# One matmul of 128 columns for two products with the same left side, transposes in place of some products with the identity, and a new step list, in a two-block transformer kernel

## The chip, the cores and the metric
The kernel runs on one core of one Trainium2 chip. The metric is the device time of one execution in microseconds (us).

## The reference
Two blocks run one after the other over 512 tokens of 1024 features in float32. The first block mixes a windowed pool with gated linear attention and has a squared-ReLU MLP. The second block has a causal convolution beside an RWKV-7 recurrence, then cross-attention to 256 memory rows, then a SwiGLU MLP. The change touches the recurrence only:

```
s_kk = einsum("bhvk,bhk->bhv", S, kk_t)
S = S * w_t[:, :, None, :] - s_kk[..., None] * (kk_t * a_t)[:, :, None, :] + v_t[..., None] * k_t[:, :, None, :]
y_t  = einsum("bhvk,bhk->bhv", S, r_t)          # 8 heads of 64, 512 steps
```

It feeds `y = concat([y_conv, y_rwkv]) @ w_out`, and the convolution has 31 taps over 512 channels.

## The kernel before
**Dense products.** All weights come as one stream of units. ScalarE rounds a unit to a high part (`wh`), VectorE takes the rest (`wl`), and every dense 128x512 product is three matmuls (`wh` by high, `wh` by low, `wl` by high). A step `mm` is half of the k range of one output tile: 12 matmuls (6 in units 76 and 77, the `wa` units). These show as `ps<-zr,wh` and `ps<-zr,wl`.

**The recurrence in chunks.** The 512 steps are 8 chunks of 64. Heads go in four pairs hp = 0 to 3; a pair has two heads (hh) on partitions 0-63 and 64-127. For each pair four groups of steps run:
- `prep.*` builds scaled keys and values. Its `prep.turn` (three steps of four 128x128 transposes) waits for the scaled arrays nB, K and P. They come from `prep.scale` and `prep.shift` on VectorE and ScalarE.
- `head.*` takes five products per chunk, each 64x64 on 64 rows: `a` (nB by P), `aa` (P by nB), `pk` (K by P), `rt` (K by R), `qt` (nB by R). VectorE masks four of them out of PSUM. Then a triangular inverse is built in five levels: `head.x` and `head.z` (64x64 by 64x32 matmuls with a VectorE op after each) and `head.tz`, which turns Z by a product with the identity (`ident`, shown as `ps<-cf_sb,zf 64*64`), after which ScalarE copies it out. Each such step is 16 matmuls, one per chunk and head; `ps<-zf 64*64` matmuls on partitions (row half, column half) of the array run four at a time. `head.gh` multiplies the inverse by two right sides, 32 matmuls.
- `fin.*` carries the state over the chunks (`fin.m`, `fin.n`, then six short dependent `fin.s`) and normalizes.
- The convolution taps: `tap.v` is one 128x512 VectorE op in PSUM (61 of them), `tap.g` a ScalarE multiply and a GpSimd add.

**What sets the order.** Each engine issues its instructions in the order of one list of steps. The list is made by `schedule()`: dense steps come in a fixed order, and at every stop the string `TURNS` says which background generator goes next (c conv taps on VectorE, g taps on GpSimd, p prep, h head pairs 0 and 2, i head pairs 1 and 3, f fin, o the `wa` and `wb` products). A dot ends the turns at one stop. After the last `p` tile (step `mm 75,1,13,1`) no dense product is left until the `wa` units. This part between them is called the bare stretch below. Steps wait on semaphores for the results that they read and for PSUM banks to be free. Background steps share five or six banks.

Every float32 matmul (not `fp32r`) is two instructions in the trace, a transpose is one. Thus a `head` step of 16 matmuls is x32 there.

Of the kernel before, what the change touches and what calls it, by code (L numbers as in the profile page):

```python
# [21 lines left out]
TURNS = """  # L22
...ppp...pp.p.p.pp.pggggp.pppp.hhggg..ccgghhcccggg.hcccc..gcc.cggghggghgccccgcc.hcccc.hcggggg.cc.hc.
h.hghc.pcghgpgpcpc..pgchcc.gpphgg.ghcc.pccpcpp.hccg..c.ghhg.hc.cpppppihggppfffgcfcffcigicpfigciciifc
pfgggiciiipicgfgiicggfcicppfpifipppcicfcpphchhhcfhhgiiggphifihhgppffffghcgghpccffchhgfcfchfcfcppfhcc
pfpchpchcfhfppcphfphpfchiicihicifiififfifcfififcfiifcicfioofiiooofooifiioiofifooffffffofofoofoofoofo
foofoofooofofoooooooo
"""
# [16 lines left out]
RO = [24, 25, 26, 27]  # L45
KS = [28, 29, 30, 31]
# [304 lines left out]
def schedule():  # L351
# [330 lines left out]
    def bg_head(z):  # L682
        for hp in (z, z + 2):
            while not has(("prep", hp)) or (z and not has(("pdone",))) or (hp >= 2 and not has(("fin", hp - 2))):
                yield

            def one(what, *more):
                for hh in range(2):
                    pl.take("M", "head." + what, hp, hh, *more)
                put("head." + what, hp, *more)  # L690
                for hh in range(2):
                    pl.rel("M", "head." + what, hp, hh, *more)
            put("head.zi", hp)
# [24 lines left out]
            yield  # L718
# [313 lines left out]
def program(nc, wstream, vecs, cf, cu, xT, metaT, memT, pmix, gup, wau, gupg, out, x2s, kvs):  # L1032
# [5 lines left out]
    with ctx:  # L1038
# [16 lines left out]
        dsm3 = sb("dsm3", [P, 24])  # L1055
        cuts = [0, 8, 24, 34, 47, 55, 75]

# [71 lines left out]
        def freed(*key):  # L1129
            k = pl.before[key]  # L1130
            if k and k[0] in ("fin.y1", "fin.yc"):
                return k[0:2]
            if k and k[0] in DIRECT:
                return DIRECT[k[0]]
            if k and k[0] == "xr.t":
                return ("xr.s", k[1][0:2], 7, 1)
            return k

# [72 lines left out]
        def cat_hl(i):  # L1211
            return R(CS[i]), R(47 + i)

        def prep_bufs(hp):

            z = hp % 3
            return (*[F(i) for i in [(3, 5, 7, 2), (4, 6, 52, 59), (21, 72, 73, 74)][z]], dsm3[:, 8 * z:8 * z + 8])

        def head_bufs(hp, hh):
            m, rest = [[(53, 54, 61, 70), (10, 11, 14, 16)], [(55, 60, 62, 63), (12, 13, 15, 17)]][hh][hp % 2], [71, 18][hp % 2]  # L1220
            (AT, AA), (Z, T), (RT, QT) = [(F(i)[:, 0:256], F(i)[:, 256:512]) for i in m[0:3]]
            return AT, AA, Z, T, F(rest)[:, 256 * hh:256 * hh + 256], RT, QT, F(m[3])

        def later(x, lv):
# [118 lines left out]
        def prods(hp):  # L1343
            return [("mm", "head." + w_, hp - 1, hh) for w_ in ("pk", "qt") for hh in range(2)] if hp else []

# [14 lines left out]
        def tensor(e):  # L1360
# [229 lines left out]

            def prod(what, lhs, rhs, hp):
                K = "head." + what
                for hh in range(2):
                    e.wait_ge(freed(K, hp, hh), *prep_done(hp))
                for _, rows_, cs, bl in CHUNKS:
                    t = [e.mm(ps(K, hp, hh)[rows_, bl], lhs[hs, cs], rhs[hs, cs]) for hh, hs in enumerate(HALVES)]
                    if bl.stop == 256 and rows_.stop == 128:
                        done2(t, K, hp)

            def head_a(hp):  # L1600
                prod("a", nB, Pp, hp)

            def head_pk(hp):
                prod("pk", F(KS[hp]), Pp, hp)

            def head_rt(hp):
                prod("rt", F(KS[hp]), F(RO[hp]), hp)

            def head_qt(hp):
                prod("qt", nB, F(RO[hp]), hp)  # L1610

            def head_aa(hp):
                prod("aa", Pp, nB, hp)
# [43 lines left out]
            def head_gh(hp, hh):  # L1657
                s0 = 64 * hh
                _, _, Z, _, PX, _, _, _ = head_bufs(hp, hh)
                b, Pt = ps("head.gh", hp, hh), prep_bufs(hp)[3]  # L1660
                e.wait_ge(freed("head.gh", hp, hh), ("head.z", hp, hh, 5), ("head.px", hp, hh))
                for a, rows_, _, bl in CHUNKS:
                    t = e.mm(b[rows_, a * 128:a * 128 + 64], Z[rows_, bl], Pt[rows_, a * 128 + s0:a * 128 + s0 + 64])
                for a, rows_, _, bl in CHUNKS:
                    t = e.mm(b[rows_, a * 128 + 64:a * 128 + 128], Z[rows_, bl], PX[rows_, bl])
                t.then_inc(*e.up("mm", "head.gh", hp, hh))

            def fin_y1(hp):
# [4 lines left out]
                for a, rows_, _, bl in CHUNKS:  # L1673
                    for hh in range(2):
                        _, _, _, _, _, _, QT, GH = head_bufs(hp, hh)
                        t = e.mm(ps("fin.y1", hp, rows_.start // 64)[64 * hh:64 * hh + 64, bl],
                                 GH[rows_, a * 128:a * 128 + 64], QT[rows_, bl])
                t.then_inc(*e.up("mm", "fin.y1", hp))
# [4 lines left out]
            def fin_m(hp):  # L1683
# [3 lines left out]
                for a, par, hh in STATE:  # L1687
                    hs, ts_, GH = HALVES[hh], HALVES[par], head_bufs(hp, hh)[7]
                    t = e.mm(ps("fin.m", hp, par)[hs, a * 64:(a + 1) * 64], GH[ts_, a * 128:a * 128 + 64],
                             nBt[ts_, a * 128 + hs.start:a * 128 + hs.stop])  # L1690
# [3 lines left out]
            def fin_n(hp):  # L1694
# [3 lines left out]
                for a in range(4):  # L1698
# [5 lines left out]
                    for par, hh in now:  # L1704
                        kc = slice(a * 128 + 64 * hh, a * 128 + 64 * hh + 64)
                        t = e.mm(ps("fin.n", hp, par)[HALVES[hh], a * 64:(a + 1) * 64], nBt[HALVES[par], kc],
                                 head_bufs(hp, hh)[7][HALVES[par], a * 128 + 64:a * 128 + 128], start=False)
                        if (a, hh) == (3 - par, 1):
# [11 lines left out]
            def fin_yc(hp):  # L1720
# [6 lines left out]
                for a, rows_, _, bl in CHUNKS:  # L1727
# [3 lines left out]
                    for hs, _, QT, GH in two:  # L1731
                        t = e.mm(o[hs, bl], GH[rows_, a * 128 + 64:a * 128 + 128], QT[rows_, bl], start=False)
                t.then_inc(*e.up("mm", "fin.yc", hp))
# [42 lines left out]
            def att_out(g, d):  # L1776
# [11 lines left out]
                "prep.gates": prep_gates, "prep.norm": prep_norm, "prep.kn": prep_kn, "prep.vmm": prep_vmm,  # L1788
                "prep.turn": prep_turn, "head.a": head_a, "head.pk": head_pk, "head.rt": head_rt, "head.qt": head_qt,
                "head.aa": head_aa, "head.tz": head_tz, "head.x": head_x, "head.z": head_z, "head.px": both(head_px),  # L1790
# [368 lines left out]
        def vector(e):  # L2159
# [317 lines left out]

            def masked(what, buf, m, hp, hh):
                K = ("head." + what, hp, hh)
                e.wait_ge(("mm", *K), *two_back(hp))  # L2480
                e.tt(c64(buf), c64(ps(*K)[:, 0:256]), half4(m), MUL).then_inc(*e.up(*K))

            def head_a(hp, hh):
                K = ("head.a", hp, hh)
                e.wait_ge(("mm", *K), ("head.zi", hp, hh))
                e.raw.copy_predicated(c64(head_bufs(hp, hh)[2]), half4("u0"), c64(ps(*K)[:, 0:256])).then_inc(*e.up(*K))

            def head_pk(hp, hh):
                masked("pk", head_bufs(hp, hh)[7][:, 0:256], "lt", hp, hh)

            def head_rt(hp, hh):
                masked("rt", head_bufs(hp, hh)[5], "le", hp, hh)

            def head_qt(hp, hh):
                masked("qt", head_bufs(hp, hh)[6], "le", hp, hh)

# [488 lines left out]
```

## Time and profile before

| | |
|---|---|
| runs (3) | 1672.67, 1674.36, 1677.11 us; median 1674.36 |
| profiled execution, its own time | 1673.94 us |
| its span, first to last instruction | 1672.0 us |
| TensorE busy (PE) | 1607.8 us, 96% |
| VectorE busy (DVE) | 820.1 us, 49% |
| ScalarE / GpSimd busy | 606.5 / 397.8 us |
| mean granted TensorE clock | 0.981 of full |

A busy PE here includes the tail of each matmul, so 96% is not 96% of its peak. The shares are means over stages; the recurrence takes about 270 of the 1672 us.

### The profile page before, as it was taken

The page shows a single profiled execution, that of the slowest core. Times are in us where ns is not written, and L with a number is a line of the kernel's source. Part 1 is how long each engine was busy: PE and PEld are TensorE (multiplying, and loading weights), DVE is VectorE, ACT ScalarE, POOL GpSimd, SP SyncE. Part 2 cuts the span into 40 slices and gives each one's busy share as a digit, 9 for nine tenths or more (in the row PEclk, how much of TensorE's full clock was granted, in tenths as well). Part 3 has the DMA queues.
Part 4 walks back from the last instruction along what each step waited for, and adds up shares of the span by engine and source line. Part 5 has one row for each costly group of instructions (what it writes and reads, how often), then busy time and mean ns, then how long its engine had stood idle before and what let it go on. Part 6 is the DMA issues. An engine that isn't in the chain of part 4 may idle for free.

```text
span 1672.0 us, 26892 instructions
## 1 busy us (share of the span) xinstructions
PE 1607.8 (96%) x11510; PEld 1316.6 (79%) x11510; DVE 820.1 (49%) x1240; ACT 606.5 (36%) x981; POOL 397.8 (24%) x333
## 2 busy tenths in 40 slices
PE   6999999999999999999999987898999999999997
PEld 5888877787888888888877766778879888888876
DVE  3376842344533333334479987637536432333334
ACT  4134432333431313234345554425335322222222
POOL 2012201302220201013317443105003430230233
PEclk8899999999999999999999999899999999999998
DMA  5122412123222222222242100014203222222212
GB/s 204 51 102 95 163 72 68 59 101 123 104 86 94 98 101 79 98 101 89 76 151 77 53 27 4 5 51 177 76 25 102 76 101 101 79 99 101 94 64 69
DMA packets 29829, 146.03 MB, mean 87 GB/s; under 512 B 4096, under 2 KB 7440, under 8 KB 14608
## 3 DMA queue, kind: packets, MB, share of 16 engines
q1 hardware_dynamic: 29712, 144.33, 24.5%
q8 instruction: 91, 1.49, 0.4%
q14 instruction: 26, 0.21, 0.0%
HBM read 138.03 MB, written 6.29 MB: 86 GB/s over the span
## 4 chain that ended last, share of the span: by engine, by line
PE 80%; issue 7%; DVE 7%; POOL 3%; ACT 2%; DMA 0%; POOLq 0%; SPq 0%; DVEq 0%
PE ps L169 79%; POOL zf L181 2%; DVE zf L181 2%; DVE ps L189 2%; DVE wl L181 1%; DVE zf L189 1%; DVE zr L189 1%; PE ps L172 1%; ACT zf L175 0%; POOL tn L181 0%; ACT zr L178 0%; DMA raw<-in_wstream 0%; ACT zf L178 0%; ACT wh L178 0%; ACT muh L178 0%
## 5 line engine op out<-in xcount | busy, mean ns | idle before, releaser
L169 PE MATMUL ps<-zr,wh 128*128 128x512 f32 (+1 forms) x3936 | 1164.5, 380 | 14.6 <-DVE wl L181 9.6
L169 PEld LDWEIGHTS ps<-zr,wh 128*128 128x128 f32 x3936 | 711.3, 188 | 170.6 <-DVE wl L181 9.8
L169 PE MATMUL ps<-zr,wl 128*128 128x512 f32 (+1 forms) x1968 | 741.6, 377 | 0.0
L181 POOL TENSOR_TENSOR zf<-zf 128x512 f32<-128x512 f32 (+1 forms) x237 | 287.8, 1220 | 804.1 <-ACT zf L175 553.4
L169 PEld LDWEIGHTS ps<-zr,wl 128*128 128x128 f32 x1968 | 370.5, 188 | 76.2
L181 DVE TENSOR_TENSOR wl<-raw,wh 128x1024 fp32r<-128x1024 f32 (+1 forms) x243 | 308.7, 1310 | 209.8 <-ACT wh L178 209.6
L178 ACT ACTIVATE wh<-raw 128x1024 fp32r<-128x1024 f32 (+1 forms) x243 | 240.4, 1038 | 211.9 <-PE ps L169 211.2
L175 ACT ACTIVATE zf<-zf 128x512 f32<-128x512 f32 (+2 forms) x232 | 127.4, 560 | 375.8 <-DVE zf L181 261.5
L181 DVE TENSOR_TENSOR zf<-ps,zf 128x512 f32<-128x512 f32 (+2 forms) x165 | 97.6, 597 | 191.9 <-PE ps L169 166.5
L169 PE MATMUL ps<-zf 64*64 64x64 f32 (+6 forms) x3768 | 167.6, 245 | 21.8 <-issue 9.8
L169 PEld LDWEIGHTS ps<-zf 64*64 64x64 f32 (+3 forms) x3768 | 131.9, 148 | 61.6 <-issue 37.3
L181 POOL TENSOR_TENSOR zr<-zf,zr 128x512 fp32r<-128x512 f32 x54 | 70.2, 1301 | 280.3 <-ACT zr L178 280.3
L178 ACT ACTIVATE zf<-ps 128x256 f32<-128x256 f32 (+2 forms) x160 | 72.6, 484 | 161.7 <-PE ps L169 149.2
L181 DVE TENSOR_TENSOR zf<-zf,ps 128x512 f32<-128x512 f32 (+2 forms) x112 | 56.5, 522 | 136.1 <-PE ps L169 135.7
L178 ACT ACTIVATE zr<-zf 128x512 fp32r<-128x512 f32 x74 | 46.6, 632 | 158.0 <-POOL zf L181 140.9
L189 DVE SCALAR_TENSOR_TENSOR zf<-ps,zf 128x512 f32<-128x512 f32 x46 | 31.5, 690 | 93.2 <-PE ps L169 87.7
L181 POOL TENSOR_TENSOR tn<-tn,cf_sb 128x2 f32<-128x2 f32 (+3 forms) x29 | 33.2, 1145 | 174.9 <-DVE tn L185 95.8
L178 ACT ACTIVATE zf<-zf,vecs_sb 128x512 f32<-128x512 f32 x73 | 50.9, 719 | 44.3 <-DVE zf L181 23.2
L189 DVE SCALAR_TENSOR_TENSOR ps<-zf,vecs_sb,ps 128x512 f32<-128x512 f32 (+1 forms) x93 | 61.0, 656 | 3.2 <-PE ps L169 2.4
L189 DVE SCALAR_TENSOR_TENSOR zr<-zf,vecs_sb,zr 128x256 fp32r<-128x256 f32 (+1 forms) x64 | 45.3, 740 | 32.5 <-ACT zr L178 32.5
L181 DVE TENSOR_TENSOR zf<-zf 128x512 f32<-128x512 f32 (+4 forms) x75 | 53.0, 720 | 10.2 <-ACT zf L175 9.8
L169 PE MATMUL ps<-cf_sb,zf 64*64 64x64 f32 (+2 forms) x860 | 43.4, 236 | 9.8 <-POOL zf L181 6.3
(95 smaller groups left out, 693.7 us busy)
## 6 DMA issues: line engine op xcount, KB each, us to landing
raw<-in_wstream SPq DMA_DIRECT2D x117, 1024.0 KB, 4.8
zf<-in_xT SPq DMA_DIRECT2D x16, 256.0 KB, 3.0
raw<-in_wstream SPq DMA_DIRECT2D x4, 768.0 KB, 4.5
kv_scratch<-zf SPq DMA_DIRECT2D x8, 256.0 KB, 2.2
x_scratch<-zf SPq DMA_DIRECT2D x8, 256.0 KB, 2.1
zf<-x_scratch SPq DMA_DIRECT2D x8, 256.0 KB, 4.1
out<-zf SPq DMA_DIRECT2D x16, 128.0 KB, 1.7
zf<-in_cu SPq DMA_DIRECT2D x1, 1256.0 KB, 10.1
```

What stands on the lines that cost most here:

```text
L169: return self.raw.matmul(out_, l, x, start=start, stop=stop)
L172: return self.raw.transpose(out_, in_, idn)
L175: return self.raw.activation(out_, in_, fn, bias=bias, scale=scale)
L178: return self.raw.activation(out_, in_, mybir.ActivationFunctionType.Copy, scale=scale)
L181: return self.raw.tensor_tensor(out_, a, b, o)
L189: return self.raw.scalar_tensor_tensor(out=out_, in0=a, scalar=s, in1=b, op0=o1, op1=o2)
```

## The change
1. `prod` now gives 128 columns for two right sides that lie in two buffers: `a` also yields `qt` (both nB on the left), `pk` also yields `rt` (both K on the left). The moving operand reads 64 columns of P and 64 of R (`beside`). VectorE masks read columns 0-63 or 64-127 of each chunk of the same bank, which is held until both masks are done. `aa` stays.
2. `head.gh` does its two right sides as one matmul of 128 columns over two buffers, 16 matmuls in place of 32. Buffers of the pairs move to make the distances positive.
3. In `head.tz` the 8 of 16 products whose output lies on partitions 0-63 become transposes.
4. `TURNS` is new. Nothing else changes in the work: masks, copies and taps are the same in number and size.

```diff
-            one("a")
-            yield
-            one("aa")
-            yield
-            one("pk")
-            yield
+            yield from two("a", "qt")
+            yield from two("pk", "rt")
+            mark("prodq", hp)
...
-                if lv < 4:
-                    one(("rt", "qt", "px")[lv - 1])
                 if lv == 2:
-                    mark("prodq", hp)
-                if lv < 4:
+                    one("px")
                     yield
...
+        def beside(c0, c1, rows_, at_=0):
+
+            x = ZF[:, c0 + at_:c0 + at_ + 64][rows_, :]
+            return bass.AP(x.tensor, x.offset, [x.ap[0], [c1 - c0, 2], x.ap[-1]])
...
             def prod(what, lhs, rhs, hp):
+
                 K = "head." + what
                 for hh in range(2):
                     e.wait_ge(freed(K, hp, hh), *prep_done(hp))
-                for _, rows_, cs, bl in CHUNKS:
-                    t = [e.mm(ps(K, hp, hh)[rows_, bl], lhs[hs, cs], rhs[hs, cs]) for hh, hs in enumerate(HALVES)]
+                for a, rows_, cs, bl in CHUNKS:
+                    to = slice(128 * a, 128 * a + 128) if len(rhs) == 2 else bl
+                    t = [e.mm(ps(K, hp, hh)[rows_, to], lhs[hs, cs],
+                              beside(*rhs, hs, cs.start) if len(rhs) == 2 else rhs[0][hs, cs])
+                         for hh, hs in enumerate(HALVES)]
...
-                    t = [e.mm(ps(K, hp, hh, lv)[HALVES[h ^ hh], bl], head_bufs(hp, hh)[2][rows_, bl],
-                              ident[rows_, rows_]) for hh in range(2)]
+                    t = [(e.mm if h ^ hh else e.tr)(ps(K, hp, hh, lv)[HALVES[h ^ hh], bl],
+                                                     head_bufs(hp, hh)[2][rows_, bl], ident[rows_, rows_])
+                         for hh in range(2)]
...
-                for a, rows_, _, bl in CHUNKS:
-                    t = e.mm(b[rows_, a * 128:a * 128 + 64], Z[rows_, bl], Pt[rows_, a * 128 + s0:a * 128 + s0 + 64])
-                for a, rows_, _, bl in CHUNKS:
-                    t = e.mm(b[rows_, a * 128 + 64:a * 128 + 128], Z[rows_, bl], PX[rows_, bl])
+                    x = (PT[hp] * 512 + a * 128 + 64 * hh, PXS[hp % 2] * 512 + 256 * hh + 64 * a)
+                    t = e.mm(b[rows_, a * 128:a * 128 + 128], Z[rows_, bl], beside(min(x), max(x), rows_))
```

The first line of `TURNS` before and now, of five:

```diff
-...ppp...pp.p.p.pp.pggggp.pppp.hhggg..ccgghhcccggg.hcccc..gcc.cggghggghgccccgcc.hcccc.hcggggg.cc.hc.
+...ppp..p..p.pp..ppp.p...cgggcccccgcpggpg.ggccpccpc..cgc.ggcchhggggh.cchch.gg.ccgghgccc.ggh.hc.ccggh
```

On TensorE, where the transposes of pair 0 (`prep.turn`, line 172) end and its first head products follow, before:

```order
L169 MATMUL ps<-zr,wl 128x512
L172 MATMUL ps<-cf_sb,zf 128x128 x12
L169 MATMUL ps<-zr,wh 128x512 x2
L169 MATMUL ps<-zr,wl 128x512
L169 MATMUL ps<-zr,wh 128x512 x2
```

and now at the place of pair 0's transposes:

```order
L172 MATMUL ps<-cf_sb,zf 128x128 x8
L169 MATMUL ps<-zr,wh 128x512 x2
L169 MATMUL ps<-zr,wl 128x512
L169 MATMUL ps<-zr,wh 128x512 x2
L169 MATMUL ps<-zr,wl 128x512
L169 MATMUL ps<-zr,wh 128x512 x2
L169 MATMUL ps<-zr,wl 128x512
L169 MATMUL ps<-zr,wh 128x512 x2
L169 MATMUL ps<-zr,wl 128x512
L172 MATMUL ps<-cf_sb,zf 128x128 x4
```

The third `prep.turn` stood directly behind the second; a dense half step of 12 matmuls lies between them now, and the transposes start three dense half steps later in the program.

On TensorE at the start of the bare stretch (the head products of pair 1 with `head.gh`, `fin.m`, `fin.n`, `fin.y1` and `fin.yc` of pair 0), before:

```order
L169 MATMUL ps<-zf 64x32 x16
L172 MATMUL ps<-cf_sb,zf 128x128 x12
L169 MATMUL ps<-zf 128x512 x2
L169 MATMUL ps<-zf 64x64 x172
L169 MATMUL ps<-cf_sb,zf 128x2 x4
```

and now:

```order
L169 MATMUL ps<-zf 64x32 x16
L172 MATMUL ps<-cf_sb,zf 128x128 x4
L169 MATMUL ps<-zf 128x512 x2
L169 MATMUL ps<-zf 64x128 x16
L169 MATMUL ps<-zf 64x64 x16
L169 MATMUL ps<-zf 64x128 x16
L169 MATMUL ps<-zf 64x64 x14
L169 MATMUL ps<-zf 64x128 x16
L172 MATMUL ps<-cf_sb,zf 64x64
L169 MATMUL ps<-cf_sb,zf 64x64 x2
L172 MATMUL ps<-cf_sb,zf 64x64 x2
```

Eight of the twelve transposes are gone from here to an earlier place. The products are 16 of 128 columns (`a` with `qt`), 16 of 64 (`aa`), 16 of 128 (`head.gh` of pair 0), 14 of 64 (`fin.m`), 16 of 128 (`pk` with `rt`); the last rows are `head.tz`, in which transposes (line 172) and products (line 169) alternate. `fin.n`, `fin.y1` and `fin.yc` come later.

On TensorE at the first dense products behind the bare stretch (`wa`, unit 76), before:

```order
L169 MATMUL ps<-zf 64x32 x16
L169 MATMUL ps<-cf_sb,zf 64x64 x16
L169 MATMUL ps<-zr,wh 128x512 x2
L169 MATMUL ps<-zr,wl 128x512
L169 MATMUL ps<-zr,wh 128x512 x2
L169 MATMUL ps<-zr,wl 128x512
L169 MATMUL ps<-zf,cf_sb 128x512
```

and now, at the end of the first dense tile:

```order
L172 MATMUL ps<-cf_sb,zf 64x64
L169 MATMUL ps<-zr,wh 128x512 x2
L169 MATMUL ps<-zr,wl 128x512
L169 MATMUL ps<-zr,wh 128x512 x2
L169 MATMUL ps<-zr,wl 128x512
L169 MATMUL ps<-zf 64x32 x16
L169 MATMUL ps<-zf 64x64 x16
L169 MATMUL ps<-zr,wh 128x512 x2
L169 MATMUL ps<-zr,wl 128x512
L169 MATMUL ps<-zr,wh 128x512 x2
L169 MATMUL ps<-zr,wl 128x512
L169 MATMUL ps<-zf,cf_sb 128x512
```

These rows are `head.z` 3 of pair 3, `fin.y` of pair 2, dense products, and `fin.mu` of pair 2. Before, pair 3 had done its levels up to `head.x` 4 and pair 2 its `fin.y` when the dense products began. Now they begin after `head.z` 2 of pair 3 and `fin.s` 5 of pair 2, so three more level steps, two turns, `fin.s` 6 and `fin.y` lie between dense products.

## Rows read from the trace of the kernel before

**Rows 1.** The page's head: span, and busy time of each engine with its instructions.

```profile
span 1672.0 us, 26892 instructions
PE 1607.8 (96%) x11510; PEld 1316.6 (79%) x11510; DVE 820.1 (49%) x1240; ACT 606.5 (36%) x981; POOL 397.8 (24%) x333
```

**Rows 2.** Windows over the recurrence: stretch, its length, then busy time by engine.

```profile
core 0: us, PE busy (x) PEld busy (x) DVE busy (x) ACT busy (x) POOL busy (x), PEclk, DMA share, GB/s
847.90:875.00 27.10, 24.78 (x128) 19.68 (x126) 19.95 (x26) 11.12 (x17) 7.90 (x5) 0.98 0.25 88
875.00:903.80 28.80, 28.80 (x354) 22.56 (x352) 22.72 (x33) 18.13 (x30) 19.53 (x14) 0.96 0.22 75
903.80:950.90 47.10, 46.22 (x506) 35.16 (x498) 44.57 (x68) 26.49 (x44) 30.95 (x19) 1.00 0.19 68
950.90:960.60 9.70, 9.70 (x108) 7.70 (x100) 8.93 (x14) 3.95 (x6) 1.30 (x1) 1.00 0.01 2
963.60:1080.20 116.60, 94.48 (x3006) 79.14 (x3005) 91.22 (x213) 57.43 (x121) 37.88 (x28) 0.93 0.02 5
1080.20:1103.70 23.50, 23.50 (x459) 18.50 (x456) 10.96 (x26) 9.51 (x19) 1.64 (x1) 1.00 0.14 48
1103.70:1118.00 14.30, 14.30 (x100) 10.40 (x96) 3.69 (x7) 5.12 (x8) 0.00 (x0) 1.00 0.19 74
```

**Rows 3.** Waits of TensorE in the bare stretch: us in total, times, longest.

```profile
PE ps L169 <- issue: 9.6, 10, 1.8
```

**Rows 4.** Timeline around pair 0's transposes, 868 to 876 us.

```profile
868.71 4.89 POOL L181 TENSOR_TENSOR zf<-zf 128x512 f32<-128x512 f32 x3
869.14 3.34 DVE L181 TENSOR_TENSOR zf<-zf 128x512 f32<-128x512 f32 x2
...
874.21 1.11 PE L172 MATMUL ps<-cf_sb,zf 128*128 128x128 f32 x4 [2.32 <-DVE zf L181]
```

**Rows 5.** Windows in which the granted clock was half: columns of rows 2.

```profile
873.80:877.20 3.40, 2.99 (x9) 2.57 (x10) 0.95 (x2) 2.41 (x5) 0.00 (x0) 0.52 0.01 5
986.60:993.30 6.70, 5.96 (x179) 5.89 (x182) 4.69 (x12) 1.13 (x4) 1.92 (x2) 0.50 0.01 2
1048.10:1054.80 6.70, 6.70 (x93) 5.53 (x92) 3.43 (x8) 2.20 (x4) 3.03 (x2) 0.50 0.01 2
1065.20:1068.30 3.10, 3.10 (x114) 3.10 (x110) 1.31 (x6) 0.00 (x0) 0.00 (x0) 0.50 0.02 5
```

**Rows 6.** Timeline of TensorE: dense products, then `head.pk` and `head.tz` of pair 0.

```profile
877.52 0.63 PE L169 MATMUL ps<-zr,wh 128*128 128x512 f32 x2
...
878.22 0.63 PE L169 MATMUL ps<-zr,wh 128*128 128x512 f32 x2
...
885.58 0.40 PE L169 MATMUL ps<-zr,wl 128*128 128x512 f32 x1
885.90 0.69 PE L169 MATMUL ps<-zf 64*64 64x64 f32 x32
886.42 0.65 PE L169 MATMUL ps<-cf_sb,zf 64*64 64x64 f32 x32
```

**Rows 7.** Timeline of TensorE, first block: four 64x64 products of 128 columns.

```profile
246.20 0.65 PE L169 MATMUL ps<-zf 64*64 64x128 f32 x8
246.78 0.50 PE L169 MATMUL ps<-zr,wh 128*128 128x512 f32 x1
```

**Rows 8.** Timeline of TensorE: full-array transposes and the product behind them.

```profile
864.81 0.60 PE L172 MATMUL ps<-cf_sb,zf 128*128 128x128 f32 x4
865.17 0.72 PE L169 MATMUL ps<-zr,wh 128*128 128x512 f32 x2
```

**Rows 9.** Groups of VectorE by form, 846 to 1118 us: busy us, mean ns.

```profile
L189 DVE SCALAR_TENSOR_TENSOR ps<-zf,vecs_sb,ps 128x512 f32<-128x512 f32 x61 | 45.7, 749 | 0.8
L181 DVE TENSOR_TENSOR zf<-ps,cu_sb 128x128 f32<-128x128 f32 x40 | 9.7, 283 | 1.9 <-PE ps L169 1.6
L181 DVE TENSOR_TENSOR zf<-zf,ps 128x128 f32<-128x128 f32 x40 | 9.6, 280 | 5.6 <-PE ps L169 5.5
```

More of the change, by code:

```diff
@@ L693, in bg_head, with two @@
             put("head.zi", hp)
-            one("a")
-            yield
-            one("aa")
-            yield
-            one("pk")
-            yield
+            def two(what, more):
+                for hh in range(2):
+                    pl.take("M", "head." + what, hp, hh)
+                put("head." + what, hp)
+                yield
+                if what == "a":
+                    one("aa")
+                    yield
+                put("head." + more, hp)
+                for hh in range(2):
+                    pl.rel("M", "head." + what, hp, hh)
+                yield
+            yield from two("a", "qt")
+            yield from two("pk", "rt")
+            mark("prodq", hp)
             one("tz", 0)
@@ L1055, in program @@
         dsm3 = sb("dsm3", [P, 24])
-        cuts = [0, 8, 24, 34, 47, 55, 75]
+        cuts = [0, 28, 34, 47, 55, 75]
         class Zone:
@@ L1136, in freed @@
                 return ("xr.s", k[1][0:2], 7, 1)
+            if k and k[0] in ("head.a", "head.pk"):
+                return ({"head.a": "head.qt", "head.pk": "head.rt"}[k[0]], *k[1:])
             return k
@@ L1343, in prods @@
         def prods(hp):
-            return [("mm", "head." + w_, hp - 1, hh) for w_ in ("pk", "qt") for hh in range(2)] if hp else []
+            return [("mm", "head." + w_, hp - 1, hh) for w_ in ("a", "pk") for hh in range(2)] if hp else []
         def both(step):
@@ L1657, in head_gh @@
             def head_gh(hp, hh):
[L1658 removed]
                 _, _, Z, _, PX, _, _, _ = head_bufs(hp, hh)
                 b, Pt = ps("head.gh", hp, hh), prep_bufs(hp)[3]
[L1661 removed]
+                e.wait_ge(freed("head.gh", hp, hh), ("head.px", hp, hh), ("head.z", hp, hh, 5))
                 for a, rows_, _, bl in CHUNKS:
[L1663 to L1665 removed]
+                    x = (PT[hp] * 512 + a * 128 + 64 * hh, PXS[hp % 2] * 512 + 256 * hh + 64 * a)
+                    t = e.mm(b[rows_, a * 128:a * 128 + 128], Z[rows_, bl], beside(min(x), max(x), rows_))
                 t.then_inc(*e.up("mm", "head.gh", hp, hh))
@@ L1688, in fin_m @@
                     hs, ts_, GH = HALVES[hh], HALVES[par], head_bufs(hp, hh)[7]
-                    t = e.mm(ps("fin.m", hp, par)[hs, a * 64:(a + 1) * 64], GH[ts_, a * 128:a * 128 + 64],
+                    t = e.mm(ps("fin.m", hp, par)[hs, a * 64:(a + 1) * 64], GH[ts_, g_at(hp, a)],
                              nBt[ts_, a * 128 + hs.start:a * 128 + hs.stop])
@@ L1706, in fin_n @@
                         t = e.mm(ps("fin.n", hp, par)[HALVES[hh], a * 64:(a + 1) * 64], nBt[HALVES[par], kc],
-                                 head_bufs(hp, hh)[7][HALVES[par], a * 128 + 64:a * 128 + 128], start=False)
+                                 head_bufs(hp, hh)[7][HALVES[par], h_at(hp, a)], start=False)
                         if (a, hh) == (3 - par, 1):
@@ L1731, in fin_yc @@
                     for hs, _, QT, GH in two:
-                        t = e.mm(o[hs, bl], GH[rows_, a * 128 + 64:a * 128 + 128], QT[rows_, bl], start=False)
+                        t = e.mm(o[hs, bl], GH[rows_, h_at(hp, a)], QT[rows_, bl], start=False)
                 t.then_inc(*e.up("mm", "fin.yc", hp))
@@ L1788, in tensor @@
                 "prep.gates": prep_gates, "prep.norm": prep_norm, "prep.kn": prep_kn, "prep.vmm": prep_vmm,
-                "prep.turn": prep_turn, "head.a": head_a, "head.pk": head_pk, "head.rt": head_rt, "head.qt": head_qt,
+                "prep.turn": prep_turn, "head.a": head_a, "head.pk": head_pk,
                 "head.aa": head_aa, "head.tz": head_tz, "head.x": head_x, "head.z": head_z, "head.px": both(head_px),
@@ L2476, in prep_shift, with masked @@
                 e.tt(Pp, kkv, TD, MUL).then_inc(*e.up("prep.P", hp))
[L2478 to L2481, printed above, removed]
+            def masked(what, of, at_, buf, m, hp, hh):
+                e.wait_ge(("mm", of, hp, hh), *two_back(hp))
+                e.tt(c64(buf), every(ps(of, hp, hh), at_), half4(m), MUL).then_inc(*e.up("head." + what, hp, hh))
             def head_a(hp, hh):
```

39 lines of the change are left out of this document (21 added, 18 removed).

## Prediction

> **What bounds the kernel now.** I read the head of the page first. TensorE is busy 1607.8 of the 1672.0 us, VectorE 820.1 us [rows 1]. The dense stages before and after the recurrence are not touched by the change, so the question is the recurrence, 847.9 to 1118 us. The windows cut it at the steps where both programs can be compared [rows 2]:
>
> - 847.9 to 875 us: dense products with the preparation of pair 0. TensorE is busy 24.78 of 27.10 us.
> - 875 to 903.8: dense, TensorE busy throughout, VectorE 22.72 of 28.80.
> - 903.8 to 950.9: dense, but VectorE is busy 44.57 of 47.10 us. VectorE is as much the bound here as TensorE.
> - 963.6 to 1080.2: the bare stretch, 116.60 us. TensorE is busy 94.48 and VectorE 91.22. Neither is full: small products and masks wait for each other. TensorE is idle 22.1 us, of which 9.6 us has no visible releaser [rows 3].
> - 1080.2 to 1118: the `wa` products. TensorE is busy all 23.50 and 14.30 us, VectorE 10.96 and 3.69.
>
> Two losses stand out. At 874.21 us the third transpose of pair 0 starts after 2.32 us of waiting for VectorE. Its inputs are late because two VectorE ops took 3.34 us together while GpSimd ran its taps (4.89 us from 868.71) [rows 4]. And in four places the granted clock was at half, the lower level of 1.2 GHz, 19.9 us together; the first place starts in that very idle time [rows 5].
>
> **Part 1, the merged products.** Sixteen products of 64 columns are 32 instructions, and from the start of `head.pk` to the start of `head.tz` behind it pass 0.52 us (885.90 to 886.42) [rows 6]. Four array quarters work side by side, so that is eight rounds of 0.065. What 128 columns cost on such a quarter stands in the first block: eight instructions on two quarters, four rounds, are 0.58 us ahead of the next dense product (246.20 to 246.78) [rows 7]. A switch of shape costs 0.09 us: dense start to 64x64 start is 0.32 us (885.58 to 885.90), where dense products follow each other at 0.70 / 3 = 0.233 [rows 6]. Without it a round of 128 columns is (0.58 - 0.09) / 4 = 0.12 us, with it 0.145; I take 0.115 to 0.12. So twice the columns cost nearly twice the time, and the number of instructions hardly counts. Per pair, before: five products of 0.52 = 2.6 us. Now: two of 8 x 0.12 = 0.95 and one of 0.52, 2.4 us. That saves 0.2 us per pair, 0.8 for four. If 128 columns cost no more than 64, it would be 1.04 per pair, 4.2 in all; at 0.145 it is a loss of 0.24 per pair, 1.0 in all. `head.gh` has 64 instructions on two quarters at a time, 32 rounds of 0.06 = 1.9 us, now 16 of 0.115 = 1.8: 0.3 us for four pairs. One or two groups less per pair between dense products save a switch of 0.09 each, 0.3 us in all. Part 1 gives **-1.4 us**.
>
> The VectorE masks are the same in number and elements and read with a stride: 0. PSUM banks are now held from the product to the second mask, which the new list must bear. If it doesn't, TensorE waits some tenths of a us for a bank. I count it in the range.
>
> **Part 2, transposes in `head.tz`.** A step is 32 instructions, in eight rounds [rows 6]. Eight of its 16 products become single instructions, so it has 24. But those on output partitions 64-127 stay products of two instructions, four on each of their two quarters: eight rounds, 0.52 us, as before. The quarters work side by side, so the transposes only shorten the two that don't end last. I take **0**. A gain of a quarter of 0.52 us, 0.13 for each of 20 steps, 2.6 us, would need the time to follow the number of instructions, which Part 1's rows speak against. The bound on the other side is a rival (below).
>
> **Part 3, the new list.** I follow the stretches.
>
> - 847.9 to 875: the three transposes of pair 0 come three dense half steps later, and the GpSimd taps start behind `prep.shift`. The 2.32 us wait has cover now: a half step is 12 x 0.233 = 2.8 us. The half clock that follows an idle TensorE [rows 5] costs up to 1.7 us; with 9 dense and transposing instructions in it I take 1.2. **-3.5 us**. If the wait comes back elsewhere: 0.
> - 875 to 903.8: 19 taps in place of 22; TensorE is the bound. 0.
> - 903.8 to 950.9: 24 taps in place of 18, six of 0.75 us = 4.5 us more on VectorE [rows 9], which had 2.5 us left. **+3.0 us** is taken (between +2.0, the overflow, and +4.5). What then waits is the dense step that needs a freed bank or a mask of `head.x` behind the taps.
> - 950.9 to 963.6: two of pair 1's transposes move here, eight transposes at 0.36 / 4 = 0.09 us or a little over, **+0.9 us** with a switch, on a full TensorE [rows 8].
> - The bare stretch: out of it go two transpose steps, `head.x` 3, `head.z` 3, `head.x` 4 and two `head.tz` of pair 3, `fin.s` 6 and `fin.y` of pair 2, and on VectorE four taps. TensorE: 0.9 + 5 x 0.5 + 1.1 = 4.5 us, less. VectorE: 4 x 0.75, six ops of 0.28 = 1.7, and about 1.0 for `fin.s` and `fin.y`, 5.7 us less of 91.22 [rows 9]. Where both take turns, the stretch follows the larger of the two: 5.7 / 91.22 x 116.6 = 7.3; purely by TensorE 4.5. I take **-6.5 us**, the saving of part 1 aside.
> - 1080.2 to 1118: the five level steps, `fin.y` and `fin.s` 6 go to where TensorE is full: 2.5 + 1.1 = **+3.5 us**, since they displace nothing idle.
>
> Hidden at no cost is the later start of pair 0's products, by dense steps; if that cover failed, pair 0 would be late for `head.gh` and the bare stretch would start with a wait of about 1 to 3 us.
>
> Sum: -1.4 + 0 - 3.5 + 3.0 + 0.9 - 6.5 + 3.5 = -4.0. The profiled execution took 1673.94 us, which gives 1669.9; the median of the runs is 0.4 higher, and I forecast **1670 us** (1665 to 1674 for this case alone).
>
> **Rivals.**
>
> *The bare stretch tightens more.* Its 22.1 us of idle TensorE and its 16.5 us at half clock [rows 2, 3, 5] are there to be won, and the order within it is new throughout. If half of the idle time and one more half-clock place go, 10 us more: **1660**. For it: neither engine is full. Against: chains of `fin.s` and the levels are as long as before, and each link needs a TensorE step, a VectorE op and two hand-overs.
>
> *The list only moves work.* The stretch keeps its length, because the chain of the levels sets it and not VectorE's sum; the dense stretches pay as above. -1.4 - 3.5 + 3.0 + 0.9 + 0 + 3.5 = +2.5: **1677**. Against it speaks VectorE at 78% of the stretch.
>
> *The transposes cost a switch each (the slower side).* In `head.tz` products and transposes now alternate, eight changes in each of 20 steps, 160 in all. If TensorE must empty at each, the nearest price is 0.09 us, that of going from full-array to 64x64 work [rows 6]: 160 x 0.09 = 14.4, so **1684**. It decides the sign from about 0.03 us a change, where it eats the 4 us. Against: in the full array the dense product behind four transposes starts 0.36 us after the first of them (864.81 to 865.17), which leaves no room for a gap [rows 8]. No row shows it for quarters. The Trainium skill speaks for this rival: "TensorEngine Tiling (Array Packing)", under Restrictions and Gotchas, says that column tiling and the transpose mode for FP32 input exclude each other on TRN2, and under Key Properties that changing the tiling mode drains TensorE. By that rule, with a gap at each change, the sum would be that of this rival; no row here shows a transpose on a quarter.
>
> **How the numbers follow.** A measurement of this kernel can tell about 0.3%, 5 us, from no change. Chances: forecast 0.43, tighter 0.20, only moved 0.22, switches 0.15. The band for same is 1669.3 to 1679.4. Faster: all of the tighter case and half of the forecast, 0.42. Slower: the switches and a little of the moved case, 0.18. Same: 0.40. The range goes from 1657 (tighter, with Part 1's and Part 2's upper gains cut) to 1684, the middle of the slow case, and leaves 0.15 outside.
>
> **What would show it.** In the profile after: TensorE has 10966 instructions (384 fewer by the merging, 160 by the transposes; if not, the change isn't what the code says). A 64x128 group of 32 takes about 0.95 us to the next start (0.52: columns are free). A `head.tz` group keeps 0.65 us (above 1 us: the switches; 0.5: the count of instructions rules). No wait of 2.3 us before a third transpose and no half clock behind it. The stretch 903.8 to 950.9 longer by 3, with waits for VectorE in dense steps. The bare stretch near 109 us. `wa` to `kt` 41 in place of 37.8. The forecast is wrong if the bare stretch keeps 116 us, or loses over 12, or if `head.tz` grows.

## The result, and the profile after

The changed kernel takes 1692.85 us (median of 4 runs, 1690.36 to 1694.72), the kernel before 1675.49 (4 runs, 1672.67 to 1677.11): 1.0096 of its time, 95% interval 1.008 to 1.0112. That is 16 us slower; the forecast was 1670, and 1684 was the end of the range.

The head of the page of the changed kernel, which answers to [rows 1]:

```profile
span 1688.4 us, 25801 instructions
PE 1636.6 (97%) x10966; PEld 1332.2 (79%) x10966; DVE 824.6 (49%) x1240; ACT 606.8 (36%) x981; POOL 395.5 (23%) x333
```

TensorE has the 10966 instructions that were foretold, 544 fewer, and is busy 28.8 us longer. So its work has become dearer. Windows over the recurrence, cut at the same steps as [rows 2] (columns of that group):

```profile
847.37:870.37 23.00, 23.00 (x115) 18.19 (x114) 14.41 (x22) 8.37 (x12) 2.40 (x2) 1.00 0.32 111
870.37:896.88 26.51, 26.51 (x205) 21.24 (x203) 25.06 (x31) 17.39 (x28) 17.82 (x13) 1.00 0.24 80
896.88:953.74 56.86, 55.49 (x567) 40.95 (x563) 51.44 (x76) 30.89 (x52) 36.27 (x25) 0.97 0.17 57
969.66:1085.73 116.07, 104.22 (x2418) 81.86 (x2417) 85.74 (x202) 55.38 (x116) 32.66 (x24) 0.91 0.01 4
1085.73:1117.07 31.34, 31.34 (x526) 23.58 (x524) 9.66 (x25) 9.15 (x18) 1.64 (x1) 0.97 0.11 35
1117.07:1133.20 16.13, 16.13 (x174) 11.63 (x168) 6.12 (x17) 4.77 (x9) 0.00 (x0) 1.00 0.20 67
```

The first stretch lost 4.1 us, the second 2.3. The third grew by 9.8, and the short one behind it (up to 966.67, the head of the next dense half step) by 3.2. The bare stretch is as long as before (116.07 against 116.60), with 588 matmuls fewer in it and 9.7 us more of busy TensorE. The `wa` stretches grew by 9.7 us together. Where this comes from shows in the timeline of TensorE at the first `head.tz` of pair 0, which answers to the `head.tz` row of [rows 6]:

```profile
902.35 0.39 PE L169 MATMUL ps<-zr,wl 128*128 128x512 f32 x1
902.67 0.24 PE L172 MATMUL ps<-cf_sb,zf 64*64 64x64 f32 x1
902.84 0.33 PE L169 MATMUL ps<-cf_sb,zf 64*64 64x64 f32 x4
903.11 0.24 PE L172 MATMUL ps<-cf_sb,zf 64*64 64x64 f32 x2
903.28 0.33 PE L169 MATMUL ps<-cf_sb,zf 64*64 64x64 f32 x4
903.54 0.25 PE L172 MATMUL ps<-cf_sb,zf 64*64 64x64 f32 x2
903.72 0.33 PE L169 MATMUL ps<-cf_sb,zf 64*64 64x64 f32 x4
903.98 0.25 PE L172 MATMUL ps<-cf_sb,zf 64*64 64x64 f32 x2
904.16 0.33 PE L169 MATMUL ps<-cf_sb,zf 64*64 64x64 f32 x4
904.42 0.24 PE L172 MATMUL ps<-cf_sb,zf 64*64 64x64 f32 x1
904.59 0.73 PE L169 MATMUL ps<-zr,wh 128*128 128x512 f32 x2
```

Line 172 is a transpose, line 169 a product. From the first transpose to the dense product behind the step pass 1.92 us, against some 0.6 before. One pair of changes takes 0.44 us (902.67 to 903.11, 903.11 to 903.54), where two rounds took 0.12. Summed over the 20 steps, the time from the first to the last start of a step is 36.7 us, against 11.1 before.

### The profile page after: what moved, and what is told of

The parts are those of the page before. It is cut to its first block, busy times and chain, and to the rows that moved or that the text cites. A ratio compares the mean times of both kernels' runs of the same rounds, so it can differ in the third digit from the quotient of the medians.

```text
span 1688.4 us, 25801 instructions
## 1 busy us (share of the span) xinstructions
PE 1636.6 (97%) x10966; PEld 1332.2 (79%) x10966; DVE 824.6 (49%) x1240; ACT 606.8 (36%) x981; POOL 395.5 (23%) x333
## 4 chain that ended last, share of the span: by engine, by line
PE 81%; issue 7%; DVE 7%; POOL 3%; ACT 2%; DMA 0%; POOLq 0%; SPq 0%; DVEq 0%; ACTq 0%
PE ps L169 79%; POOL zf L181 2%; DVE zf L181 2%; DVE ps L189 2%; PE ps L172 2%; DVE zf L189 1%; DVE wl L181 1%; DVE zr L189 1%; ACT zr L178 0%; ACT zf L175 0%; POOL tn L181 0%; ACT wh L178 0%; DMA raw<-in_wstream 0%; ACT zf L178 0%; DVE zr L181 0%
## 5 line engine op out<-in xcount | busy, mean ns | idle before, releaser
L181 DVE TENSOR_TENSOR wl<-raw,wh 128x1024 fp32r<-128x1024 f32 (+1 forms) x243 | 314.0, 1332 | 208.3 <-ACT wh L178 208.2
L169 PE MATMUL ps<-zf 64*64 64x32 f32 (+8 forms) x3384 | 165.2, 254 | 15.8 <-DVE zf L181 6.2
L169 PEld LDWEIGHTS ps<-zf 64*64 64x64 f32 (+3 forms) x3384 | 128.4, 149 | 57.5 <-issue 32.8
L178 ACT ACTIVATE zf<-ps 128x512 f32<-128x512 f32 (+2 forms) x160 | 73.5, 484 | 190.0 <-PE ps L169 175.6
L169 PE MATMUL ps<-cf_sb,zf 64*64 64x64 f32 (+2 forms) x540 | 56.6, 252 | 9.4 <-POOL zf L181 6.9
L169 PEld LDWEIGHTS ps<-cf_sb,zf 64*64 64x64 f32 (+1 forms) x540 | 45.2, 164 | 17.8 <-POOL zf L181 9.3
```

The costliest lines, as they stand in the source:

```text
L169: return self.raw.matmul(out_, l, x, start=start, stop=stop)
L178: return self.raw.activation(out_, in_, mybir.ActivationFunctionType.Copy, scale=scale)
L181: return self.raw.tensor_tensor(out_, a, b, o)
```

## The experiments

All times are medians; each ratio is against the kernel before in the same comparison (its medians 1676.4 to 1677.9 us). The four kernels of the first comparison take the change apart.

**1. The products back.** Of the changed kernel only the transposes are undone:

```diff
-                    t = [(e.mm if h ^ hh else e.tr)(ps(K, hp, hh, lv)[HALVES[h ^ hh], bl],
-                                                     head_bufs(hp, hh)[2][rows_, bl], ident[rows_, rows_])
-                         for hh in range(2)]
+                    t = [e.mm(ps(K, hp, hh, lv)[HALVES[h ^ hh], bl], head_bufs(hp, hh)[2][rows_, bl],
+                              ident[rows_, rows_]) for hh in range(2)]
```

> The changed kernel with all sixteen turns of each inverse step as products again; merged products and the new step list stay. Theory (each change between transpose and product costs): a turning step falls from 1.92 to about 0.6 us, 20 of them are 26 us less work on TensorE; some of it lay where TensorE waited anyway, so 1692.9 falls to 1668 to 1674 us. Rival (the new list or the merged products lose the time and the long turning steps lie beside waits): 1685 to 1693 us.

Measured: 1674.05 us, 0.9979 (0.9969 to 0.9988). The transposes alone make the difference between 0.9979 and 1.0096, 19.6 us (18.8 between the medians). Its `head.tz` at the same place, on TensorE's timeline, takes 0.62 us again:

```profile
903.45 0.69 PE L169 MATMUL ps<-cf_sb,zf 64*64 64x64 f32 x32
904.07 0.73 PE L169 MATMUL ps<-zr,wh 128*128 128x512 f32 x2
```

**2. The transposes alone.** The kernel before, with the same edit of `head.tz` the other way round.

> The kernel before with the transposes in its turning steps as the only edit. Theory: 20 steps times 1.3 us is 26 us more; the bare stretch before has 22 us of idle TensorE that may hide some, so 1675.5 rises to 1692 to 1702 us, more than the whole change did. Rival (list or merging is to blame): 1675 to 1680 us.

Measured: 1690.59 us, 1.0082 (1.0069 to 1.0095), 13.8 us slower, a little under what was expected. The steps sum to 37.5 us from first to last start, 26.4 more than before. TensorE's waits between 847 and 1135 us are 12 us in all, against 24 before, so nearly half of the added work fell into time in which it had been idle.

**3. Transposes first, then products.**

```diff
+                for op, d in ((e.tr, 0), (e.mm, 1)):
+                    for a in range(4):
+                        t = []
+                        for hh in range(2):
+                            h = hh ^ d
+                            rows_, bl = HALVES[h], slice(64 * a, 64 * a + 64)
+                            t.append(op(ps(K, hp, hh, lv)[HALVES[h ^ hh], bl],
+                                        head_bufs(hp, hh)[2][rows_, bl], ident[rows_, rows_]))
```

> The changed kernel with the eight transposes of a turning step first and the eight products behind them: two changes of kind in a step in place of eight or nine, the same instructions. If a change of kind costs 0.16 us: a step takes 0.24 us for the transposes, 0.47 for the products on two quarters and 0.3 for two changes, about 1.0 us, and the time is 1674 to 1681 us. If each 64-column transpose is slow by itself: the step stays near 1.9 us and the time near 1692 us.

Measured: 1679.6 us, 1.0011 (1.0003 to 1.002). One change in a step in place of eight; timeline of TensorE:

```profile
903.82 0.41 PE L172 MATMUL ps<-cf_sb,zf 64*64 64x64 f32 x8
904.17 0.68 PE L169 MATMUL ps<-cf_sb,zf 64*64 64x64 f32 x16
904.78 0.74 PE L169 MATMUL ps<-zr,wh 128*128 128x512 f32 x2
```

The step takes 0.95 us, still 0.33 more than products alone, so the number of changes isn't the whole price. In this order the transposes would stand in rounds of their own in any case; that the two kinds don't run side by side shows where they alternate. There a product starts 0.17 us after the transposes ahead of it (903.11 to 903.28), while in experiment 1 four products start within 0.02 us of each other.

**4. The list alone.** Experiment 1 with each product of 128 columns issued as two of 64 in its place, `head.gh` too:

```diff
+                    if len(rhs) == 2:
+                        for m in range(2):
+                            t = [e.mm(ps(K, hp, hh)[rows_, 128 * a + 64 * m:128 * a + 64 * m + 64], lhs[hs, cs],
+                                      ZF[:, rhs[m] + cs.start:rhs[m] + cs.start + 64][hs, :])
+                                 for hh, hs in enumerate(HALVES)]
```

> As the first of these (turns as products, new list), but each merged product of 128 columns is two of 64 columns into the same places of the bank, for the head products and for the inverse times its right sides. So only the new list is left of the change. If time goes with columns: 0.92 us for a merged group against 1.0, 1.70 against 1.86 for the inverse, 0.3 us per pair and 1.4 us in all more than the first run. If the number of instructions counts: 4 us or more above the first run.

Measured: 1676.4 us, 0.9998 (0.999 to 1.0007). The new list by itself gives nothing, and the merging on it 2.3 us, between the two expectations. With intervals of 0.1% (some 1.6 us) on each side, it can't be told from 1.4.

**5. The merging alone, on the old list.** `TURNS` is that of before; `head.qt` and `head.rt` are masks directly behind `head.a` and `head.pk`:

```diff
+            def two(what, more):
...
+                put("head." + what, hp)
+                put("head." + more, hp)
...
+            two("a", "qt")
             yield
-            one("a")
```

> The list of steps of the kernel before, head.tz as products, and only the merged products (head.a with head.qt, head.pk with head.rt, head.gh as one of 128 columns); each second mask stands directly behind the first. This is Part 1 alone. By the runs so far (the merging took 2.3 us off the new list) it should be 1.4 to 2.5 us under the kernel before, with five products of 0.52 us per pair replaced by two of 0.93 and one of 0.52. Rival: the bank that is now held for two masks makes TensorE wait on the old list, and the time is that of before or up to 2 us more.

Measured: 1670.32 us, 0.9956 (0.9942 to 0.997). That is 6.9 us faster, three to five times what was expected, so something else than columns is at work here.

**6 and 7. Transposes only where TensorE is full, or only where it isn't.** The changed kernel, with transposes in the 8 steps between dense products (below), or in the other 12 (the condition without its `not`):

```diff
-                    t = [(e.mm if h ^ hh else e.tr)(ps(K, hp, hh, lv)[HALVES[h ^ hh], bl],
+                    t = [(e.mm if h ^ hh or not (hp == 0 or (hp == 3 and lv > 1)) else e.tr)(ps(K, hp, hh, lv)[HALVES[h ^ hh], bl],
```

> The changed kernel with transposes only in the 8 head.tz steps that lie between dense products (all five of pair 0, the last three of pair 3), products in the other 12. Theory: the 1.30 us that a step grows is paid in full where TensorE is always busy, 8 x 1.30 = 10.4 us over the run with products (1674.05), so 1684. Rival, each step costs the same wherever it stands (18.8 us / 20): 7.5 us, 1681.5.

> The counterpart: transposes only in the 12 head.tz steps of the bare stretch. Theory: 12 x 1.30 = 15.6 us more work of TensorE, of which its idle time there (23.8 us in the run with products, 13.7 in the changed kernel) takes up some 8 to 10, so 6 to 8 us over 1674.05: 1680 to 1682. Rival, the same per step wherever it stands: 11.3 us, 1685.

Measured: 1680.81 us, 1.002 (1.0011 to 1.0029), for the 8 steps, and 1689.25, 1.0072 (1.0051 to 1.0093), for the 12. My theory fell: the first is at the rival's 1681.5, and the second is dearer than either said. TensorE's waits, as in experiment 2, are 23.8 us in the run with products, 22.9 with the 8 and 18.2 with the 12. So some cover exists in the bare stretch, 5.6 us, and hardly any in the dense ones, 0.9. But the runs also differ in how long the granted clock was at half in the recurrence: 20.4 us with the 8 steps, 30.6 with the 12 and with products. And the four executions with the 12 steps spread with their mean clock: 1686.1 and 1687.0 us at 0.978 and 0.976, 1691.5 and 1695.4 at 0.973 and 0.969. What one step costs by its place can't be read out of these.

**8. Full array.** In the kernel before, every second transpose of `prep.turn` is a product with the identity:

```diff
+                    t = (e.mm if tt % 2 else e.tr)(ps("prep.t", hp, c)[:, cs], (nB, F(KS[hp]), Pp)[c][:, cs], ident)
...
```

The dots stand for the signal behind the loop.

> The kernel before; in its prep.turn steps (full-array tiles of 128 by 128) every second transpose is a product with the identity instead, so that transposes and products alternate there, three changes in each of 12 steps. Theory that only quarters pay for a change: a step in a dense stretch takes two transposes and two products of two instructions at 0.109 us each, six rounds, about 0.65 us to the next start, and no start-to-start gap is over 0.12 but at the first. Rival, a change between product and transpose costs in any shape: gaps of 0.15 us or more at each change, a step of 1 us or more. The whole time within 3 us of before either way.

Measured: 1673.95 us, one run. Timeline of TensorE at the first of these steps:

```profile
871.31 0.27 PE L172 MATMUL ps<-cf_sb,zf 128*128 128x128 f32 x1
871.42 0.39 PE L169 MATMUL ps<-cf_sb,zf 128*128 128x128 f32 x2
871.64 0.27 PE L172 MATMUL ps<-cf_sb,zf 128*128 128x128 f32 x1
871.75 0.39 PE L169 MATMUL ps<-cf_sb,zf 128*128 128x128 f32 x2
871.97 0.27 PE L172 MATMUL ps<-cf_sb,zf 128*128 128x128 f32 x1
```

A transpose and the two instructions of a product come every 0.33 us (871.31, 871.64, 871.97), three times 0.11. On the full array the changes cost nothing. Of the two shapes tried only the 64x64 quarters pay.

**9. Three changes.** The changed kernel with `head.tz` as 4 transposes, 4 products, 4 transposes, 4 products; it is the loop of experiment 3 in two parts:

```diff
+                for n in (0, 2):
+                    for op, d in ((e.tr, 0), (e.mm, 1)):
+                        for a in (n, n + 1):
```

> The changed kernel with head.tz in four groups: 4 transposes, 4 products, 4 transposes, 4 products, so three changes in a step, between the one of the grouped run (0.95 us to the next start) and the eight of the changed kernel (1.92). Theory of two parts: transposes don't run beside products of the other quarters, which costs 0.22 us a step whatever the order, and each change costs 0.12 to 0.13 more, so 0.60 + 0.22 + 3 x 0.125 = 1.20 us a step. Rival, changes alone at 0.16 each: 0.60 + 0.48 = 1.08. The time lies a third of the way from the grouped run to the changed kernel, near 1684.

Measured: 1684.95 us, 1.0034 (1.0016 to 1.0053). Timeline of TensorE:

```profile
903.15 0.30 PE L172 MATMUL ps<-cf_sb,zf 64*64 64x64 f32 x4
903.38 0.45 PE L169 MATMUL ps<-cf_sb,zf 64*64 64x64 f32 x8
903.76 0.30 PE L172 MATMUL ps<-cf_sb,zf 64*64 64x64 f32 x4
904.00 0.45 PE L169 MATMUL ps<-cf_sb,zf 64*64 64x64 f32 x8
904.37 0.73 PE L169 MATMUL ps<-zr,wh 128*128 128x512 f32 x2
```

1.22 us a step; the theory of two parts said 1.20, the rival 1.08. With 0, 1, 3 and 8 changes a step takes 0.62, 0.95, 1.22 and 1.92 us. A straight line through these gives 0.14 for each change, and 0.19 once, when there are transposes at all.

The starts of the single matmuls, which the rows above merge, show the two parts more closely. Inside a run of one kind a new round starts every 0.056 us (transposes) or 0.058 us (products). From the last of one kind to the first of the other pass 0.145 to 0.149 us, 0.09 more, and the second round behind a change comes 0.08 or 0.10 us after the first, 0.02 to 0.04 more. So a change costs 0.11 to 0.13 us, and four rounds of transposes 0.22.

The whole time, 1684.95 where 1684 was expected, shows less than the step. Four of the six executions ran at a mean clock of 0.974 or 0.975 (1684.6 to 1686.7 us); the two at 0.980 and 0.983 took 1680.1 and 1676.7. The changed kernel's ran at 0.976 to 0.978.

**10. The same order as in 5, unmerged.** Experiment 5 with the edit of experiment 4.

> The same order as in the run with merged products on the old list, but each product of 128 columns is issued as two of 64 in the same place. It parts what the merging did there (6.9 us) into order and columns. If it is the columns and instructions alone, this is back at the kernel before, 1677. If it is that head.rt and head.qt no longer stand inside the chain of the levels in the bare stretch, with the columns worth 2.3 us as on the new list, it is 1672.6.

Measured: 1677.77 us, 1.0006 (0.9998 to 1.0015). So the order gave nothing; the merging itself is worth 0.5%, 7 to 8 us. The clock doesn't explain it: at a mean clock of 0.980 the merged kernel took 1669.7 and 1670.0 us, the unmerged one 1676.4. The waits of TensorE between 962 and 1085 us (us in total, times, longest) show where, first of this kernel:

```profile
PE ps L169 <- issue: 10.1, 10, 1.9
```

and of the merged one:

```profile
PE ps L169 <- issue: 2.7, 2, 1.6
```

These are the waits with no visible releaser, 9.6 us before [rows 3]. All but 2 of 10 are gone, 7.4 us. What goes with them shows in the kernel before. Timeline of TensorE from 1020 us:

```profile
1020.82 1.39 PE L169 MATMUL ps<-zf 64*64 64x64 f32 x73
1024.00 0.82 PE L169 MATMUL ps<-zf 64*64 64x64 f32 x34 [1.80 <-issue]
...
1026.80 1.08 PE L169 MATMUL ps<-zf 64*64 64x64 f32 x53
1028.97 1.01 PE L169 MATMUL ps<-zf 64*64 64x64 f32 x47 [1.10 <-issue]
```

and the share of the DMA engines from 1020 to 1032, in slices of 0.3 us:

```profile
DMA  0000020000000000000001000000000002000000
```

In these 12 us three packets move, each 16 KB of instructions. The first two start at 1021.5 and 1026.6 and land at 1022.67 and 1027.53, and the waits end at 1024.00 and 1028.97. By the times of these packets in the trace, each of the eight longer `issue` waits of the kernel before ends 1.21 to 1.49 us after such a load has landed, and the ten of the unmerged run end 1.19 to 1.54 us after. I take it that TensorE runs out of instructions there. Not every load brings a wait: none follows the third one here. In the bare stretch of the kernel before 23 such loads came, one every 4.9 us, for 6011 matmuls and weight loads [rows 2], about 260 a load. The Trainium skill, "Runtime: NRT & Kernel Launch", section "Instruction fetch mechanics", describes a FIFO refilled in 16 KiB blocks of 256 instructions and calls the cost of crossing a boundary mostly hidden. The trace agrees on the size of a block. On the cost it doesn't if these waits are for instructions: 9.6 us in 117, where small matmuls follow each other closely. The number of instructions doesn't decide it alone. Experiment 4 has as many as experiment 10 and lost 0.9 us to such waits, not 10.1; there TensorE waited more for VectorE (21.7 us over the recurrence, 12.6 before), time in which a load may land.

**11. One move of the new list, on top of 5.** In the first line of `TURNS`:

```diff
-pggggp.pppp.hhggg..ccgghh
+pggggp.pp.pp.hhggg.ccgghh
```

> The merged products on the old list (1670.3 us), and of the new list one move only: the third prep.turn of pair 0 stands one dense half step later, and with it the first head products. Theory: the 2.3 us wait before it and the half clock behind it (from 874.5) go, 3.5 to 4 us as in the changed kernel, so 1666.5 to 1667. Rival: the time comes back later, since pair 0 goes on half a dense step later and VectorE bounds the stretch behind (903.8 to 950.9); then 1669 to 1671.

Measured: 1669.41 us (1664.98 to 1672.54), 0.9954 (0.9939 to 0.9969). Timeline of TensorE at the third `prep.turn` of pair 0, which now waits for nothing, against [rows 4]:

```profile
873.97 0.39 PE L169 MATMUL ps<-zr,wl 128*128 128x512 f32 x1
874.20 0.60 PE L172 MATMUL ps<-cf_sb,zf 128*128 128x128 f32 x4
```

Locally the theory holds: 847.5 to 871.3 us is 23.8 us in place of 27.1, no half clock follows, and up to the bare stretch nothing is given back. The profiled execution was the fastest of the six, though, and the medians differ by 0.9 us with intervals that overlap. Of 3.3 us no more than this can be told in the whole. This and experiment 5 beat both kernels, by 0.4 to 0.5% against before.

**12. Instructions without work.** Experiment 5 with waits that have long been met: 8 ahead of each chunk of `head.a` and `head.pk`, 4 ahead of each of `head.gh`'s products.

```diff
+                    if len(rhs) == 2:
+                        e.again(8, "in.cf")
...
+                    e.again(4, "in.cf")
```

> The merged products on the old list (1670.3 us), with 192 waits per pair added to TensorE's program in head.a, head.pk and head.gh, on a semaphore that has long reached its value. They do no work in the array but stand in the stream of instructions: about 768 entries, as many as the merging took out. Theory: what the merging won on the old list is that TensorE runs out of instructions less often (the idle times that no engine ends, 10.1 us in the unmerged run against 2.7, all end 1.2 to 1.6 us after a load of 16 KB of instructions has landed). Then the loads in the stretch rise by about 3, these idle times come back by several us, and the time goes 3 to 8 us up, towards 1677. Rival: what counts is the time in the array; then the added waits cost nothing beside the products and the time stays within 1.5 us of 1670.3.

Measured: 1699.28 us, 1.0133 (1.0114 to 1.0152), 29 us over experiment 5. Both theories missed. Timeline of TensorE, `head.a` and `head.aa` of pair 0:

```profile
876.93 3.53 PE L175 MATMUL ps<-zf 64*64 64x128 f32 x64
880.39 0.73 PE L175 MATMUL ps<-zr,wh 128*128 128x512 f32 x2
```

The two steps take 3.46 us, 1.50 in experiment 5: each of 64 waits, eight in a row, costs 0.03 us where it stands, which would be 23 us for 768. Over the recurrence the `issue` waits are 5.9 us against 2.7, the direction expected, but the effect that was meant to be isolated lies under a larger one. That fewer instructions (and not fewer passes through the array) end the `issue` waits rests on their timing and on the pair 5 and 10; a run that changes the number of instructions alone is missing.

## Why the prediction was wrong, step by step

**Part 2 failed, and with it the sign.** The step reads "The quarters work side by side, so the transposes only shorten the two that don't end last. I take 0." Measured: +19.6 us, or +13.8 on the old list. Transposes on quarters don't run beside products on the others: they take rounds of their own, and each change between the two costs time. By the line through the four kinds of step that is 0.19 + 8 x 0.14 = 1.31 us a step, 26 us for 20. Of that, TensorE's waits took up 10: they are 23.8 us with products and 13.6 in the changed kernel. That leaves 16 us. The recurrence is 15.4 us longer, 300.3 us against 284.9. These are the two profiled executions, which differ by 14.8 us in the whole; the medians differ by 4 us more, and no trace shows where.

The rival of the switches was right in its mechanism, and its 0.09 us is what a change adds between the last start of one kind and the first of the other. I took it from the way from dense to quarter work [rows 6]. The way out has the same price: from the last quarter product to the next dense one pass 0.15 us in the trace of before (886.85 to 886.99), where quarter rounds follow each other at 0.06. What the rival lacked is the slower first round behind each change and the rounds of the transposes themselves. In the changed kernel's step that is 8 x 0.09 = 0.72 us of gaps, 0.26 of slower rounds and 0.28 for five rounds of transposes, 1.26 of the 1.30 us measured. And [rows 8], which I held against it, show the full array; experiment 8 confirms them there, and they say nothing on quarters. The rule that I cited, that column tiling excludes the FP32 transpose mode ("TensorEngine Tiling (Array Packing)" in the Trainium skill, Restrictions and Gotchas), is met in part. 160 transposes of 64x64 run here, so it doesn't hold as a ban; but where the two kinds alternate, none runs beside a product. That TensorE empties at each change, as this rival supposed, fits the gap of 0.15 us, the same as between quarter and dense work. The traces show the gap and not its reason. I gave this rival 0.15.

**Part 1, right in its prices, wrong in its size.** A 128-column group was to take 0.95 us:

```profile
895.85 1.10 PE L169 MATMUL ps<-zf 64*64 64x128 f32 x32
896.88 0.72 PE L169 MATMUL ps<-zr,wh 128*128 128x512 f32 x2
```

That is `head.pk` of pair 0 in the changed kernel, 1.03 us to a dense product and 0.92 to another group: nearly twice the time for twice the columns, as said. What failed is the term for the whole of part 1, -1.4 us, which counts time in the array alone. On the new list the merging gave 2.3 us, which may still be 1.4; on the old one 7.4 between the medians, and there 7.4 us of `issue` waits went with it. The 9.6 us of [rows 3] were on the table, and I used them only as idle time to be won by order. Whether it is the number of instructions that ends these waits stays open (experiment 12).

**Part 3, near in the sum, by luck in its terms.** Experiments 1 and 4 show it without the transposes. Stretches of experiment 1 against before, predicted in brackets: -4.1 (-3.5), -2.3 (0), +6.2 (+3.0), +3.5 (+0.9) for the short one at 950.9, -7.6 (-6.5 and part 1), +4.6 (+3.5). The bare stretch, cut as in [rows 2], is 107.8 us there (968.40 to 1076.15), near the forecast of 109. The dense stretches pay more than I took, above all 903.8 to 950.9, where VectorE has the taps. By the ratio the list with the merging gives -0.21%, 3.5 us, where -4.0 stood. But the stretches add up to +0.3 us, since the profiled execution of before was a quick one (1673.94 us, with a median of 1677.25 beside experiment 1) and that of experiment 1 was not (1675.58, median 1674.05). So they show where the list gives and takes, and don't show the 3.5 us. The list alone gives nothing (0.9998), and on the merged kernel it costs some 4 us (experiments 1 and 5). It turned the `issue` waits (0.9 us in experiment 4, 9.6 before) into waits for VectorE: TensorE's waits over the recurrence are 27.5 us in all, against 24.2 before.

**The wait and the half clock at 874** went as predicted. The half clock came back at other places: 20.4 us in the recurrence before, 27.2 in the changed kernel, 30.6 in experiment 1.

## What to carry to other kernels

Before mixing two kinds of matmul on quarters of the array, look for a row in which they alternate on quarters; a row on the full array doesn't answer for it. An instruction count that falls is no gain in itself, as 160 fewer made each step three times as long. But where the waits of an engine have no releaser and stand between many small instructions, fewer and larger ones can be worth more than their time in the array: 7.4 us against 1.4 on the old list, though hardly on the new one. Which of two orders is better can turn with that, so compare them again.

## What the runs showed of the hardware

- On 64x64 tiles float32 transposes and products don't overlap. A change costs 0.11 to 0.13 us by the single starts (0.14 by the line through four kinds of step), and eight transposes in four pairs 0.22 us (0.19 by the line). On 128x128 tiles a change costs nothing (0.11 us from start to start throughout).
- Instructions come in loads of 16 KB that take 0.9 to 1.4 us. In the bare stretch of before TensorE stood still 10 times in 117 us, for 0.2 to 1.8 us each, and went on 1.2 to 1.6 us after such a load had landed. That it waited for instructions is read from this timing; no run isolates it.
- Waits that are already met, eight in a row ahead of small matmuls, cost TensorE about 0.03 us each.
